# A two-layer decoder trunk: x is transposed and split without its norm, and the roots enter at the copies out of PSUM

## What is computed

```python
def rms_norm(x, g):
    y = xf * lax.rsqrt(jnp.mean(xf * xf, axis=-1, keepdims=True) + EPS) * g.astype(jnp.float32)

# layer A: stick-breaking attention, 16 heads of 64
h = rms_norm(x, norm_g)
q, k, v, gate = jnp.split(h @ w_in, 4, axis=-1)
x = x + (silu(gate) * stick_breaking_attention(q, k, v)) @ w_out
# layer B: keys and values from the new x, then differential attention, 8 heads
h = rms_norm(x, kv_norm_g);  k, v = jnp.split(h @ w_kv, 2, axis=-1)
k = apply_rope(rms_norm(k, k_norm_g), cos, sin)
h = rms_norm(x, norm_g);     q, gate = jnp.split(h @ w_in, 2, axis=-1)
x = x + (silu(gate) * rms_norm(differential_attention(q, k, v), subln_g)) @ w_out
```

## Time and profile before

| | |
|---|---|
| runs | 647.70, 647.96, 650.90 us; median 647.96 |
| profiled execution | 647.47 us, of which the span of the trace is 646.2 us |
| TensorE / its weight loads busy | 623.3 us (96%) / 525.6 us (81%) |
| VectorE / ScalarE / GpSimd busy | 448.2 us (69%) / 334.4 us (52%) / 352.2 us (54%) |
| chain that ended last | TensorE 65%, VectorE 20%, ScalarE 8%, issue 4% |

### The profile page before, as it was taken

One profiled execution on the slowest core, in us unless ns is written; L12 is line 12 of the kernel. 1 busy time (PEld: TensorE's weight loads), 2 busy tenths in 40 slices (PEclk: granted clock), 3 DMA queues, 4 the chain that ended last, 5 costly groups with the idle time before them and its releaser, 6 DMA issues.

```text
span 646.2 us, 9996 instructions
## 1 busy us (share of the span) xinstructions
PE 623.3 (96%) x3324; PEld 525.6 (81%) x3324; DVE 448.2 (69%) x701; ACT 334.4 (52%) x728; POOL 352.2 (54%) x339
## 2 busy tenths in 40 slices
PE   5999999999999999999998999999899999999998
PEld 4788778888888888888887888788688888887786
DVE  3486177979788797983327298605779999998541
ACT  5342184676747667584316625424456645576320
POOL 5556396546565555743541454447575775556161
DMA  7433122112131220211211322222322220221142
GB/s 260 107 101 98 50 83 81 49 50 65 37 91 38 62 65 32 81 51 53 67 61 34 106 95 93 81 82 67 102 78 66 81 76 13 74 83 66 32 135 93
DMA packets 61774, 49.08 MB, mean 76 GB/s; under 512 B 7729, under 2 KB 48817, under 8 KB 61745
## 3 DMA queue, kind: packets, MB, share of 16 engines
q1 hardware_dynamic: 58064, 48.25, 24.3%
q10 hardware_dynamic: 3680, 0.46, 0.5%
HBM read 44.50 MB, written 2.10 MB: 72 GB/s over the span
## 4 chain that ended last, share of the span: by engine, by line
PE 65%; DVE 20%; ACT 8%; issue 4%; DMA 1%; SPq 0%; DVEq 0%; POOL 0%; ACTq 0%
PE bank L593 17%; PE bank L595 16%; PE bank L594 16%; PE bank L707 6%; ACT pr L1318 4%; PE bank L721 3%; PE bank L692 3%; DVE hi L1483 2%; DVE small L1680 2%; DVE pr L1701 1%; DVE at_lo L1735 1%; DVE h_hi L1446 1%; DVE v L1398 1%; DVE lo L1488 1%; DVE qs L1629 1%
## 5 line engine op out<-in xcount | busy, mean ns | idle before, releaser
L471 POOL TENSOR_TENSOR w_lo<-w_raw,w_hi 128x512 fp32r<-128x512 f32 x60 | 82.2, 1377 | 120.4 <-ACT w_hi L1015 120.4
L483 POOL TENSOR_TENSOR w_lo<-w_raw,w_hi 128x512 fp32r<-128x512 f32 x100 | 143.3, 1433 | 8.0
L481 POOL CAST w_hi<-w_raw 128x512 fp32r<-128x512 f32 x100 | 75.7, 757 | 129.5 <-DVE pr L1701 35.7
L593 PE MATMUL bank<-h_hi,w_hi 128*128 128x512 f32 x320 | 129.3, 404 | 2.1 <-ACT q L1227 2.0
L593 PE MATMUL bank<-w_hi,h_hi 128*128 128x512 f32 x320 | 128.3, 401 | 2.9 <-DVE h_lo L1404 2.8
L595 PE MATMUL bank<-w_hi,h_lo 128*128 128x512 f32 x320 | 125.7, 393 | 0.0
L594 PE MATMUL bank<-w_lo,h_hi 128*128 128x512 f32 x320 | 125.6, 392 | 0.0
L595 PE MATMUL bank<-h_hi,w_lo 128*128 128x512 f32 x320 | 125.4, 392 | 0.0
L594 PE MATMUL bank<-h_lo,w_hi 128*128 128x512 f32 x320 | 125.1, 391 | 0.0
L593 PEld LDWEIGHTS bank<-w_hi,h_hi 128*128 128x128 f32 x320 | 60.7, 190 | 16.0 <-DVE h_lo L1404 3.5
L593 PEld LDWEIGHTS bank<-h_hi,w_hi 128*128 128x128 f32 x320 | 60.1, 188 | 16.5 <-ACT q L1227 1.9
(11 more groups left out here) (174 smaller groups left out, 1194.6 us busy)
## 6 DMA issues: line engine op xcount, KB each, us to landing
w_raw<-in_a_w_in SPq DMA_DIRECT2D x64, 256.0 KB, 2.7
w_raw<-in_w_kv SPq DMA_DIRECT2D x32, 256.0 KB, 3.1
w_raw<-in_b_w_in SPq DMA_DIRECT2D x32, 256.0 KB, 2.8
w_raw<-in_a_w_out SPq DMA_DIRECT2D x16, 256.0 KB, 2.7
w_raw<-in_b_w_out SPq DMA_DIRECT2D x16, 256.0 KB, 3.0
xs<-in_x SPq DMA_DIRECT2D x4, 512.0 KB, 4.8
qrot<-qs SPq DMA_DIRECT2D x32, 64.0 KB, 2.0
out_x<-xs SPq DMA_DIRECT2D x8, 256.0 KB, 2.6
```

Source lines behind the costliest of these rows:

```text
L471: nc.gpsimd.tensor_tensor(w_lo[s][:, :], w_raw[s][:, :], w_hi[s][:, :].bitcast(F32), ALU.subtract).then_inc(s_w, 1)
L481: nc.gpsimd.tensor_copy(w_hi[s][:, :], w_raw[s][:, :]).then_inc(s_whi, 1)
L483: nc.gpsimd.tensor_tensor(w_lo[s][:, :], w_raw[s][:, :], w_hi[s][:, :].bitcast(F32), ALU.subtract).then_inc(s_w, 1)
L593: pe.matmul(o, ahi, bhi, start=start, stop=False, skip_group_check=True)
```

## The change

- x itself is transposed, as it lands from memory (layer A) or as the residual is added (layer B), and multiplied by the gain only. `h2` holds these parts, not normed, in both layers.
- V, and in layer B keys and values, come out of products with `h2`, and the copies out of PSUM multiply each row by its root.
- Queries, keys of layer A and all gates use `h1`, which must be normed: TensorE transposes the roots, spread over 128 columns, into one bank (`turn_roots`), ScalarE copies it to `og` (`roots_copy`) and keeps a full copy of each transposed tile (`input_raw`, `sum_raw`), VectorE multiplies (`query_scale`), ScalarE rounds (`query_hi`), VectorE subtracts (`query_lo`).
- ScalarE copies the first half of V between the fourth and fifth of these roundings, and its V slabs 10, 11 and 12 are spread among them.
- Layer B: the first four tiles are transposed after the second step of the output projection's second half, the others after the third step of keys; the banks of layer B's groups follow a list (`KV_BANK`).
- All small transfers are issued by ScalarE ahead of everything else. `keep_busy` stands only between the first transposes.

```diff
@@ -83,11 +83,14 @@
-BUSY_A, BUSY_B = 30, 14
-SPLITS_B = [(0, 0), (1, 0), (0, 1), (2, 0), (1, 1), (3, 0), (2, 1), (3, 1),
-            *((k, to) for k in range(4, KT) for to in (0, 1))]
+BUSY_A = [4, 8, 4, 8]
+TURN_BANK = [7, 6, 1, 2, 4, 5, 0, 3]
+KV_BANK = [1, 2, 6, 7, 0, 3, 4, 5, 1, 2, 0, 3, 4, 5, 1, 2]
+KV_PRIOR = {n: max(m for m in range(n) if KV_BANK[m] == KV_BANK[n]) for n in range(8, 16)}
...
@@ -626,20 +631,18 @@
 -        def turn_input(k0, k1, n, done):
...
+        def turn_input(k, t):
+            tr = pe.transpose(bank[4 + k % 4][:, cols(t * P, P)], xs[:, t, cols(k * P, P)], ident[:, :])
+            if t == TT - 1:
+                tr.then_inc(s_tp, 1)
+        def turn_roots(n, o):
+            pe.wait_ge(s_rx, n + 1)
             for t in range(TT):
+                tr = pe.transpose(o[:, cols(t * P, P)], rx[:, t:t + 1].to_broadcast([P, P]), ident[:, :])
+            tr.then_inc(s_rt, 1)
...
@@ -650,20 +653,33 @@
-        keep_busy(neg_one[:, :], BUSY_A)
-        turn_input(0, 4, 0, 0)
+        for t in range(TT):
+            pe.wait_ge(s_x[t], 16)
+            for k in range(4):
+                turn_input(k, t)
+            keep_busy(neg_one[:, :], BUSY_A[t])
...
                 elif k == 0:
-                    pe.wait_ge(s_h, KT)
+                    pe.wait_ge(s_raw, KT)
                 if v_slab(half * KT + k) == G_QK0 + 4:
+                    pe.wait_ge(s_h, 2 * KT)
                     project(G_QK0, h1_hi, h1_lo, bank[7][:, :])
-                bulk_step(v_slab(half * KT + k), half * TT, k, h1_hi, h1_lo, s_vk, 0)
-                if half == 0 and k < 4:
-                    turn_input(k + 4, k + 5, 0, k + 1)
+                bulk_step(v_slab(half * KT + k), half * TT, k, h2_hi, h2_lo, s_vk, 0)
+                if half == 0 and k < 3:
+                    pe.wait_ge(s_raw, k + 1)
+                    for t in range(TT):
+                        turn_input(k + 4, t)
+                if half == 0 and k == 3:
+                    pe.wait_ge(s_raw, 4)
+                    turn_roots(0, bank[7])
+                if half == 0 and k == 4:
+                    pe.wait_ge(s_rc, 1)
+                    for t in range(TT):
+                        turn_input(7, t)
...
@@ -781,13 +797,18 @@
+        def turn_sum(half, tiles=range(TT)):
+            for k in (half * TT + n for n in tiles):
+                for t in range(TT):
+                    pe.wait_ge(s_x2, half * TT + t + 1)
+                    tr = pe.transpose(bank[TURN_BANK[k]][:, cols(t * P, P)], xs[:, t, cols(k * P, P)], ident[:, :])
+                tr.then_inc(s_tp, 1)
         for k in range(KT):
             bulk_step(G_OUT + KT + k, TT, k, h2_hi, h2_lo, banks_of=OUT_BANK_A)
-        pe.wait_ge(s_x2, TT)
-        keep_busy(h2_hi[:, 0, :], BUSY_B)
-        turn_input(0, 4, 1, 0)
...
@@ -814,21 +835,39 @@
+        def kv_step(grp, k):
+            if k:
+                bulk_step(kv_slab(grp * KT + k), 4 * grp, k, h2_hi, h2_lo, banks_of=KV_BANK)
+                return
+            for t in range(TT):
+                if grp >= 2:
+                    pe.wait_ge(s_vk, V_BY_ACT + KV_PRIOR[4 * grp + t] + 1)
+                bulk_step(kv_slab(grp * KT), 4 * grp, 0, h2_hi, h2_lo, banks_of=KV_BANK, tiles=(t,))
...
-                    pe.wait_ge(s_h, split_no(1, k, 0))
-                elif k == 0:
-                    pe.wait_ge(s_h, 3 * KT)
+                    pe.wait_ge(s_h, 2 * KT + k + 1)
+                    if k == 0:
+                        pe.wait_ge(s_raw, KT + TT)
+                if grp == 1 and k == 0:
+                    pe.wait_ge(s_raw, 2 * KT)
+                    pe.wait_ge(s_rc, 2)
                 if kv_slab(grp * KT + k) == H_Q0 + 2:
+                    pe.wait_ge(s_h, 4 * KT)
                     pe.wait_ge(s_kc, KT)
                     project(H_Q0, h1_hi, h1_lo, bank[6][:, :])
-                bulk_step(kv_slab(grp * KT + k), 4 * grp, k, h2_hi, h2_lo, s_vk, V_BY_ACT)
+                kv_step(grp, k)
                 if kv_slab(grp * KT + k) == H_Q0 + 2:
                     sums(q=0)
-                if grp == 0 and k < 4:
-                    turn_input(k + 4, k + 5, 1, split_no(1, k, 1))
+                if grp == 0 and k == 2:
+                    turn_roots(1, bank[3])
+                    turn_sum(1, range(3))
+                    pe.wait_ge(s_rc, 2)
+                    turn_sum(1, (3,))
...
@@ -1021,20 +1053,28 @@
-        def split_input(n, k, to):
-            act.wait_ge(s_tp, n * KT + k + 1)
-            if to:
-                act.wait_ge(s_h, split_no(1, k, 0))
-            g, dst = (0, h1_hi) if n == 0 else ((1, h2_hi), (2, h1_hi))[to]
-            A(dst[:, k, :], bank[4 + k % 4][:, :], ACT.Copy, scale=gain[:, g, k:k + 1]).then_inc(s_hh, 1)
-        nc.scalar.preload_act_table_set("natural_log_exp_and_others")
-        for t in range(TT):
-            squares(0, t, 0)
-            squares(0, t, 1)
-        root(tiny[:, 0:4], tiny[:, 4:8], R_A)
-        norm_last_rows(0)
+        def input_hi(k):
+            act.wait_ge(s_tp, k + 1)
+            A(h2_hi[:, k, :], bank[4 + k % 4][:, :], ACT.Copy, scale=gain[:, 0, k:k + 1]).then_inc(s_hh, 1)
+        def input_raw(k):
+            act.wait_ge(s_h, k + 1)
+            A(raw_input(0, k), bank[4 + k % 4][:, :], ACT.Copy, scale=gain[:, 0, k:k + 1]).then_inc(s_raw, 1)
+        def roots_copy(n, src):
+            act.wait_ge(s_rt, n + 1)
+            A(og[:, :], src[:, :], ACT.Copy).then_inc(s_rc, 1)
+        def query_hi(n, k):
+            act.wait_ge(s_f, n * KT + k + 1)
+            A(h1_hi[:, k, :], (g32, ge)[k % 2][:, :], ACT.Copy).then_inc(s_hh, 1)
+        with nc.allow_non_contiguous_dma(reason="one column per feature tile"):
+            nc.scalar.dma_start(gain[:, 0, :], a_norm_g.rearrange("o (k p) -> p (o k)", p=P)).then_inc(s_gain, 16)
...
+        load_params()
+        nc.scalar.preload_act_table_set("natural_log_exp_and_others")
+        for t in (0, 1):
+            squares(0, t, 0)
+            squares(0, t, 1)
         act.wait_ge(s_gain, 16)
+        for k in range(4):
+            input_hi(k)
+        for k in range(4):
+            input_raw(k)
+        for t in (2, 3):
+            squares(0, t, 0)
+            squares(0, t, 1)
+        root(tiny[:, 0:4], tiny[:, 4:8], R_A)
+        for k in range(4, KT):
+            input_hi(k)
+            if k == 6:
+                roots_copy(0, bank[7])
+            input_raw(k)
+            slab_hi(v_slab(RING_A + k - 4))
+        def values_a(n):
+            bulk_tile(act, v_slab((n // TT + 1) * KT - 1) + 1, n)
+            A(v32[:, n % TT, cols(n // TT * HALF, HALF)], bank[n % 6][:, :], ACT.Copy,
+              scale=rx[:, n % TT:n % TT + 1]).then_inc(s_vk, 1)
         for k in range(KT):
-            split_input(0, k, 0)
+            query_hi(0, k)
+            if k == 1:
+                slab_hi(v_slab(10))
             if k == 3:
-                load_params()
-            if k >= 4:
-                slab_hi(v_slab(RING_A + k - 4))
+                for n in range(TT):
+                    values_a(n)
+                slab_hi(v_slab(11))
+            if k == 5:
+                slab_hi(v_slab(12))
...
-        for n in (10, 11, 12):
-            slab_hi(v_slab(n))
-        for n in range(TT):
-            values_a(n)
         slab_hi(v_slab(13))
...
@@ -1195,16 +1255,24 @@
-        for t in range(TT):
-            squares(1, t, 1)
-        root(tiny[:, 0:4], tiny[:, 4:8], R_B)
-        norm_last_rows(1)
+        def sum_hi(k):
+            act.wait_ge(s_tp, KT + k + 1)
+            act.wait_ge(s_wu, G_OUT + KT + k + 1)
+            A(h2_hi[:, k, :], bank[TURN_BANK[k]][:, :], ACT.Copy, scale=gain[:, 1, k:k + 1]).then_inc(s_hh, 1)
+        def sum_raw(k):
+            act.wait_ge(s_h, 2 * KT + k + 1)
+            A(raw_input(1, k), bank[TURN_BANK[k]][:, :], ACT.Copy, scale=gain[:, 2, k:k + 1]).then_inc(s_raw, 1)
...
-        for k, to in SPLITS_B:
-            split_input(1, k, to)
-            if k >= 4 and to:
-                kv_hi(k)
-        kv_hi(8, 9, 10)
+        for k in range(TT):
+            sum_hi(k)
+        for k in range(TT):
+            sum_raw(k)
+        for t in range(TT):
+            squares(1, t, 1)
+        kv_hi(4)
+        root(tiny[:, 0:4], tiny[:, 4:8], R_B)
+        kv_hi(5)
+        roots_copy(1, bank[3])
+        for k in range(TT, KT):
+            sum_hi(k)
+        query_hi(1, 0)
+        kv_hi(6)
+        query_hi(1, 1)
+        sum_raw(4)
+        sum_raw(5)
+        kv_hi(7)
+        query_hi(1, 2)
+        sum_raw(6)
+        sum_raw(7)
+        query_hi(1, 3)
+        kv_hi(8)
+        query_hi(1, 4)
+        kv_hi(9)
+        query_hi(1, 5)
+        query_hi(1, 6)
+        kv_hi(10)
         for n in range(4):
             bulk_copy(n)
+        key_square(0)
+        key_square(1)
         kv_hi(11)
-        for n in range(4):
-            key_square(n)
+        query_hi(1, 7)
         kv_hi(12)
+        key_square(2)
+        key_square(3)
```

(49 more changed lines are left out.)

52 lines of the change are left out of this document (16 added, 36 removed).

## The result

The changed kernel took **655.88 us** in the median of four executions (655.41 to 658.16), the kernel before 647.87 beside it: a ratio of 1.0127, 95% interval 1.0103 to 1.0151. It is 8 us slower, where 645.9 was forecast with a range up to 650.0. The profiled execution took 655.41, its span is 654.1 us, against 646.2.

What follows compares the result with a forecast made beforehand. TensorE, busy 96% of the span, was taken as the bound. Start 0.2 plus seam 1.9 gave 2.1 us, from a median of 647.96 to 645.9; the range reached from the case in which the covers hold to 650.

Steps and rivals of the forecast that it cites:

- ScalarE's issues end at 10.4: Start, head of ScalarE's queue: transfer issues end at 10.4 us, so the first product comes at 15.6, 4.1 earlier.
- the 1.6: Start: 1.60 us that one issue behind two gains took in the old run; the worst case took it twice.
- the slower rival: Start: issues pushed back by x end at 14, TensorE may return at 1.2 GHz; 5.2 us slower, 653.2; chance 0.15.
- Slab 14: Start, late in layer A's V: slab 14 ready at 72.7, TensorE there at 69.2, so it stands 3.5 us.
- The clock behind the waits: After TensorE stands 3 us or more: nine products at 0.43 for 0.23 us, 1.8 us, in one rival only.
- Start as a whole: Start of layer A: net gain of 0.2 us, between 3.3 with no collisions and minus 1.8.
- Seam, the gain: Between the layers: keys and values follow the output projection at once, 5.62 us, less 0.44 for transposes; minus 5.2.
- Seam, what it gives back: Between the layers: key chain 4.8 us later against TensorE; loss 3.3 us, between 1.8 and 5.0.
- The covers hold: Rival, start and seam: GpSimd's work misses nearly all sixteen operations; gains 3.3 and 3.4, 641.3 us; chance 0.27.
- All goes back: Rival, both places: the key chain takes all 5.2 us and the angles all of the start; 647.9; chance 0.13.
- signs of being wrong: V's end moves over 3 us, TensorE doesn't wait at either place, or the first product is later than 18.
- The page on SBUF: VectorE and GpSimd's shared port: a collision costs up to 1.3 us, start minus 1.0; the sum used 1.0 each.

Runs made afterwards that it cites:

- run 4: Changed kernel with SP holding back x's four transfers and the slabs until the 15 small transfers had landed; one execution, 662.61 us.
- run 10: Changed kernel with the eighth query rounding before the key copies, KV slabs 13, 14 before the key roots, 15, 16 after the first key tile; 653.31 us.
- run 1: Changed kernel with the 14 parameter transfers issued by SP after V's sixth slab; 649.6 us, ratio 1.0025 to the kernel before.
- run 6: Changed kernel with ScalarE rounding V's slabs 14 and 15 before the sines; 657.51 us, ratio 1.0135 to the kernel before.

## Why the prediction was wrong, step by step

- **ScalarE's issues end at 10.4: wrong, the step that failed.** They ended at 16.37. The sum took 8.4 us from the row of before and added 0.5 for the third gain and one stall of 1.2; alone they even take less than I said (8.0, run 4). Missing was the product of two things, single elements and the start's large transfers beside them, worth 7 us. The worst that this sum allowed, about 13 with twice the 1.6, was not bad enough, nor was the slower rival's 14. From the issues' true end the sum holds: 1.3 + 2.4 + 1.5 behind 16.4 gives 21.6, and 21.66 came.
- **Slab 14: right.** The angles began 35.5 us after the first product (34.9 forecast), and TensorE waited 3.24 (3.5). Both shifted with the first product, so this term is a loss by itself.
- **The clock behind the waits: left out of the sum.** It stood only in the slower rival, at 1.8 us once. It was 1.4 at slab 14 and 1.4 at the keys. The "some 6 us" that TensorE was to stand ahead of the first product doesn't fit the forecast either: its fillers ended at 13.87, 1.7 before the 15.6 of the sum, and the true stop was 7.80.
- **Start as a whole:** a gain of 0.2 us was forecast, and the first mask came 7.4 later. Of these 7.6, 6.1 are the first product (21.66 for 15.6) and 1.4 the clock.
- **Seam, the gain: right.** The gap closed, 5.9 us with the move of the transposes (5.6 forecast), less 0.44 for the roots. Roots and later tiles were in time.
- **Seam, what it gives back: mis-sized.** TensorE waited 4.58 at the first keys and not at all at the second; I had 3.1 and 0.3 (which make 3.4, not the 3.3 of the text). Up to the first tile the forecast was near: by the same subtraction as in the prediction the first group ended at 368.63 and the tile began 11.5 us later, 4.4 more than before, where 4.8 was forecast. But it took the tile itself as it had been (4.9 us, 374.12 to 379.06 in the earlier trace rows); the tile met four splits and took 6.93. With the clock's 1.4 behind it the seam gave −0.5, not 1.9.
- **The rivals.** *The covers hold* fell, since TensorE waited at both places. *All goes back* had the seam nearly right, but not the start. The slower one was the right mechanism at both its points, the head of the queue and the clock, and its 653.2 was still too low. It got 0.15; its evidence against, issues of 0.5 us at 18.17, was taken from a moment when x had long landed. That row could not speak for the first 10 us. Two of the signs of being wrong came, the first product later than 18 and V's end more than 3 us off.
- **The page on SBUF.** The Trainium skill, "SBUF — State Buffer", section "SBUF: two separate sides", gives the shared port to whichever instruction starts first, for the whole of it, and by the prediction's reading a collision then costs up to GpSimd's 1.3 us. Four splits cost 4.11 us (6.93 in the changed kernel, 2.82 in run 10), 1.03 each, as in the rows of before. That lies under the bound, so the trace agrees with the page, and the 1.0 of the rows was the right price for the sum.

In one sentence: the change bought 5.9 us at the seam, and paid 7.4 at the start, which without the loads at the head of ScalarE's queue would have been 0.7 (first mask of run 1 at 80.08), and 6.4 from the first keys on.

Open: what in the queues holds the single elements back was not traced, nor how much of it is x and how much V's first slabs, and the seam alone, on the old start, was not run.

## What to carry to other kernels

Count a transfer's issue time by what else is in flight when it is issued, and never put loads of single elements ahead of the engine work that opens the pipeline: here 15.5 us against 8.0. When operations with two SBUF operands are added to VectorE, look at what GpSimd does in the same stretch, then at what stands behind them in every in-order queue; moving GpSimd's work earlier can take more from VectorE than the wait that it removes. TensorE's waits of 3.2 and 4.6 us cost their length and 1.4 us each behind them, which products that nobody reads win back. A wait that moves to another place takes this with it: in run 6 it grew to 4.75 us and cost 2.3 behind it.
